# Dilated attention in a two-block kernel: score tiles by residue modulo 4, two slots in one unit of work

## What is computed

```python
for g, (window, dilation) in enumerate(DIL_GROUPS):        # (128, 1), (512, 4), (2048, 16)
    hs = slice(g * HEADS_PER_GROUP, (g + 1) * HEADS_PER_GROUP)
    o, lse = dilated_window_attention(q_d[:, hs], k_d[:, hs], v_d[:, hs], window, dilation)
    outs.append(o)
    lses.append(lse)
w_grp = jax.nn.softmax(jnp.stack(lses, axis=0), axis=0)
o_dil = jnp.sum(w_grp[..., None] * jnp.stack(outs, axis=0), axis=0).astype(h.dtype)
...
o_sb = stick_breaking_attention(qkv_s[0], qkv_s[1], qkv_s[2])
y = gate_dil * (o_dil @ w_proj_dil) + gate_sb * (o_sb @ w_proj_sb)
return y @ w_out
```

## Time and profile before

| | us |
|---|---|
| median of 3 runs | 2889.4 (2888.75 to 2892.43) |
| profiled execution | 2897.6 |
| its span, first to last instruction | 2895.8 |
| PE busy | 2758.5 (95%) |
| DVE busy | 1407.1 (49%) |
| ACT busy | 990.7 (34%) |
| POOL busy | 195.5 (7%) |
| TensorE clock granted, mean of the span | 0.976 |

### The profile page before, as it was taken

The page is one execution under the profiler, slowest core; times in us unless marked ns, Lnnn a source line. Parts: engine busy times, 40 slices in busy tenths (PEclk is TensorE's granted clock), DMA queues, the critical chain, the costliest instruction groups (busy, mean ns, idle before and its releaser), DMA issues.

```text
span 2895.8 us, 30679 instructions
## 1 busy us (share of the span) xinstructions
PE 2758.5 (95%) x12252; PEld 2158.3 (75%) x12252; DVE 1407.1 (49%) x1944; ACT 990.7 (34%) x1367; POOL 195.5 (7%) x149
## 2 busy tenths in 40 slices
PE   7997986999999999989999999999999998999998
PEld 6876764888877766668888888888776666788886
DVE  5455985434454344274443554434544434543434
ACT  5444864222231222453222332223312235422222
POOL 0000115000005000010000000000230001000000
PEclk9997997999999999899999999999999999999999
DMA  4128962222232111032222232222321100322222
GB/s 140 54 71 291 419 265 94 95 95 95 91 105 81 66 50 32 8 100 95 95 95 95 86 104 95 95 95 82 108 81 58 44 19 26 116 95 95 95 95 73
DMA packets 86399, 289.03 MB, mean 100 GB/s; under 512 B 10014, under 2 KB 15070, under 8 KB 86254
## 3 DMA queue, kind: packets, MB, share of 16 engines
q1 hardware_dynamic: 79406, 262.81, 26.6%
q0 software_dynamic: 6272, 22.12, 2.0%
q10 hardware_dynamic: 576, 2.10, 0.2%
HBM read 274.40 MB, written 12.58 MB: 99 GB/s over the span
## 4 chain that ended last, share of the span: by engine, by line
PE 90%; DVE 4%; ACT 3%; issue 2%; DMA 1%; POOL 0%; SPq 0%; DVEq 0%; ACTq 0%; POOLq 0%
PE bank_l L442 73%; PE bank_s L1744 2%; PE bank_o L1761 2%; PE bank_l L1185 2%; PE bank_s L1185 1%; DVE w_lo L416 1%; PE bank_t L1772 1%; PE bank_t L442 1%; PE bank_s L1797 1%; PE bank_s L1742 1%; ACT w_hi L411 1%; PE bank_t L1710 1%; PE bank_s L1811 1%; PE bank_o L1826 1%; PE bank_s L1815 1%
## 5 line engine op out<-in xcount | busy, mean ns | idle before, releaser
L442 PE MATMUL bank_l<-xg_hi,w_hi 128*128 128x512 f32 (+1 forms) x2192 | 879.6, 401 | 18.5 <-DVE w_lo L416 14.4
L442 PE MATMUL bank_l<-xg_lo,w_hi 128*128 128x512 f32 (+1 forms) x2192 | 863.9, 394 | 0.0
L442 PE MATMUL bank_l<-xg_hi,w_lo 128*128 128x512 f32 (+1 forms) x2192 | 858.5, 392 | 0.0
L416 DVE TENSOR_TENSOR w_lo<-w_raw,w_hi 128x1024 fp32r<-128x1024 f32 (+2 forms) x441 | 532.0, 1207 | 227.0 <-ACT w_hi L411 224.9
L411 ACT ACTIVATE w_hi<-w_raw 128x1024 fp32r<-128x1024 f32 (+2 forms) x441 | 435.6, 988 | 434.0 <-PE bank_l L442 418.7
L442 PEld LDWEIGHTS bank_l<-xg_hi,w_hi 128*128 128x128 f32 x2192 | 417.0, 190 | 136.8 <-issue 26.0
L442 PEld LDWEIGHTS bank_l<-xg_lo,w_hi 128*128 128x128 f32 x2192 | 416.1, 190 | 98.2 <-issue 8.4
L442 PEld LDWEIGHTS bank_l<-xg_hi,w_lo 128*128 128x128 f32 x2192 | 417.0, 190 | 90.7
L442 PE MATMUL bank_l<-hid_lo_ff,w_hi 128*128 128x512 f32 x704 | 278.5, 396 | 0.0
L442 PE MATMUL bank_l<-hid_hi_ff,w_lo 128*128 128x512 f32 x704 | 278.5, 396 | 0.0
L442 PE MATMUL bank_l<-hid_hi_ff,w_hi 128*128 128x512 f32 x704 | 278.5, 396 | 0.0
(11 more groups left out here) (331 smaller groups left out, 2821.4 us busy)
## 6 DMA issues: line engine op xcount, KB each, us to landing
w_raw<-in_ff_gate SPq DMA_DIRECT2D x88, 512.0 KB, 3.2
w_raw<-in_ff_up SPq DMA_DIRECT2D x88, 512.0 KB, 3.2
expert_raw<-in_experts SPq DMA_DIRECT2D x81, 512.0 KB, 6.6
w_raw<-in_in SPq DMA_DIRECT2D x80, 512.0 KB, 3.2
w_raw<-in_ff_down SPq DMA_DIRECT2D x64, 512.0 KB, 3.2
w_raw<-in_out SPq DMA_DIRECT2D x24, 512.0 KB, 3.3
w_raw<-in_ff_down SPq DMA_DIRECT2D x32, 384.0 KB, 3.0
y_rows<-y_slot_tile POOLq DMA_DIRECT2D x16, 512.0 KB, 6.6
```

What stands on the lines that cost most here:

```text
L416: dve.tensor_tensor(w_lo[:, i % SPLIT, 0:kc * cols], panel_memory(i), w_hi[:, i % SPLIT, 0:kc * cols].bitcast(F32), ALU.subtract).then_inc ...
L442: done = pe.matmul(dst, w[:, i % SPLIT, c * cols:(c + 1) * cols], moving, start=c == 0 and n == 0, stop=c == kc - 1 and n == 2)
```

## The change

A unit is now a **pair** of slots and a block of queries: eight units for each layer instead of sixteen, with two fillers in each. Within a block of 128 queries the tokens of the second and third group are ordered by their residue modulo 4 (four classes of 32), and the keys and values of these groups by residue over the whole sequence (four classes of 128). A query reads only keys of its own class, so its scores in such a group are one tile of 128, whatever the block. The scores of a slot now fill one bank of 512: 256 keys of the first group, 128 each of the second and third.

- PE: no mask matmuls. For the first group one matmul of 256 columns for each slot of the pair (z = 0, 1), for the others 16 matmuls with 64 rows, 32 columns of weights and 128 columns moving, alternating between the two slots, each to its own 32 partitions of the bank.
- DVE adds a mask in fp32 (`far_masks`, 1 MB, loaded by POOL's queue at the start of each mixer) and takes the maximum in one `tensor_tensor_reduce` for each slot, from PSUM to `prob`. It is built as two instructions. The weights are no longer scaled: the heads are (`take_heads`).
- ACT takes one exponential of 512 for each slot, from SBUF, and copies the weights of z = 0 out of PSUM; DVE copies those of z = 1.
- PE transposes eight blocks (six in the first block) in a row. Its value matmuls have the weights stationary and 64 columns of values moving, so the heads come out token by token: for each slot two of 128 weight columns and eight of 32 weight columns, each with its own 32 partitions. The values of unit u-2 stand behind the transposes of unit u-1. Odd and even units have PSUM banks of their own.
- The heads go to `o_tok` (memory of `squares`). After the last unit the first stick-breaking head waits for it, and PE turns them back with eight transposes (`turn_heads`) behind that head's filler. ACT and DVE split them there (`round_heads`, `rest_of_heads`). The stick-breaking heads are split straight from `bank_o` one by one. `o_f` is gone.
- POOL writes the product with `cos` to a buffer of its own (`turning`), and adds ten of the twelve chunks in the order of the classes: it reads contiguously and writes 32 or 128 elements apart. DVE takes four of the value panels in that order too.
- The bf16 masks of the program's start shrink from 11 tiles to one, and a matmul of one column (L1817) is gone.

```diff
...
-        o += [(f"in_{l}", i) for i in (*range(18), 22, 23, *range(18, 22), *range(24, 40))]
+        o += [(f"in_{l}", i) for i in (*range(18), 22, 23, 18, 24, 19, 25, 20, 26, 21, *range(27, 40))]
...
-            o_f = sb(phase, "o_f", [P, 4, T])
...
+                far_masks = sb(att, "far_masks", [P, TB, T])
...
+                    turning = sb(rope, "turning", [P, 2, T])
...
+                        prob = sb(dilated, "prob", [P, 4, T])
+                        prob_t = sb(dilated, "prob_t", [P, 4, T])
+                    spent = sb(work, "spent", [P, 2, 1280])
...
+            o_tok = squares[:, :, :].rearrange("p a (b d) -> p (a b) d", d=2 * P)
...
-        units = [(s, blk) for blk in range(TB) for s in range(SLOTS)]
+        units = [(pair, blk) for blk in range(TB) for pair in range(SLOTS // 2)]
...
+        def near_keys(blk):
+            return max(blk - 1, 0) * P
...
-                for g in range(3):
-                    pe.matmul(bank_s[:, g, 0:w], ident_bf[:, :], masks_f[:, MASK_END[g] - w:MASK_END[g]],
-                              start=True, stop=False)
-                    m = pe.matmul(bank_s[:, g, 0:w], qk[po:po + 64, ch, blk * P:(blk + 1) * P],
-                                  qk[po:po + 64, 6 + ch, k0 * P:(blk + 1) * P], start=False, stop=True)
...
+                    pe.wait_ge(*routed.upto(("peak", l, u - 1, 1)))
+                for z in range(2):
+                    rows = slice(64 * z, 64 * z + 64)
+                    pe.matmul(bank_s[:, z, 0:2 * P], qk[rows, pair, blk * P:(blk + 1) * P],
+                              qk[rows, 6 + pair, near_keys(blk):near_keys(blk) + 2 * P], start=True, stop=True)
+                for g in (1, 2):
+                    for c in range(4):
+                        for z in range(2):
+                            rows, at = slice(64 * z, 64 * z + 64), blk * P + 32 * c
+                            m = pe.matmul(bank_s[32 * c:32 * c + 32, z, (g + 1) * P:(g + 2) * P],
+                                          qk[rows, 2 * g + pair, at:at + 32],
+                                          qk[rows, 6 + 2 * g + pair, c * P:(c + 1) * P], start=True, stop=True)
...
-                for j in range(nb):
-                    m = pe.matmul(bank_o[po:po + 64, 0:P], v2_tok[:, k0 + j, head:head + HEAD],
-                                  prob_t[:, y, j * P:(j + 1) * P], start=g == 1 and j == 0, stop=g == 0 and j == nb - 1)
...
+            def turn_weights(u):
+                pair, blk = units[u]
+                for z in range(2):
+                    pe.wait_ge(*func.upto(("exp", l, u, z)))
+                    t = claim(pe, t_banks, ("pt", l, u, z), turned_out_v if z else turned_out, ("pt", l, u, z))
+                    for j in range(4):
+                        if blk or j != 1:
+                            m = pe.transpose(t[:, j * P:(j + 1) * P], prob[:, 2 * (u % 2) + z, j * P:(j + 1) * P],
+                                             ident[:, :])
+                    m.then_inc(*turned.done(("pt", l, u, z)))
...
+                    dst, weights = out_bank(u)[:, 64 * z:64 * z + 64], prob_t[:, 2 * (u % 2) + z, :]
+                    head = (2 * pair + z) * HEAD
+                    pe.wait_ge(*(turned_out_v if z else turned_out).upto(("pt", l, u, z)))
+                    for j in range(min(blk, 1) + 1):
+                        pe.matmul(dst, weights[:, j * P:(j + 1) * P],
+                                  v2_tok[:, near_keys(blk) // P + j, head:head + HEAD],
+                                  start=j == 0, stop=False, skip_group_check=True)
+                    for g in (1, 2):
+                        for c in range(4):
+                            at = (g + 1) * P + 32 * c
+                            m = pe.matmul(dst[32 * c:32 * c + 32, :], weights[:, at:at + 32],
+                                          v2_tok[:, c, 256 * g + head:256 * g + head + HEAD],
+                                          start=False, stop=g == 2, skip_group_check=True)
...
+            for u in range(n_units):
+                dilated_scores(u)
+                for n in (2 * u, 2 * u + 1):
+                    x_product(pe, filler(l, n), taken, filler(l, n))
                 if u:
-                    dilated_values(u - 1)
-            weigh_values(*owed.pop())
+                    turn_weights(u - 1)
+                if u >= 2:
+                    weigh_values(u - 2)
+            turn_weights(n_units - 1)
...
+            def turn_heads(pair):
+                t = claim(pe, t_banks, ("heads", l, pair), split_lo, ("o", l, pair))
+                pe.wait_ge(*taken.upto(("o", l, n_units - 1)))
+                for blk in range(TB):
+                    m = pe.transpose(t[:, blk * P:(blk + 1) * P], o_tok[:, blk, pair * P:(pair + 1) * P], ident[:, :])
+                m.then_inc(*turned.done(("heads", l, pair)))
...
-                pe.matmul(bank_s[:, 2, 0:1], ident_bf[:, :], masks_f[:, 0:1], start=False, stop=True,
-                          skip_group_check=True).then_inc(*mixed.done(("weights", l, h)))
...
+            def exp_scores(u):
+                for z in range(2):
+                    act.wait_ge(*routed.upto(("peak", l, u, z)))
+                    st, p = stat[:, u % 2, :], prob[:, 2 * (u % 2) + z, :]
+                    act.activation(p, p, ACT.Exp, scale=-1.0, bias=st[:, z:z + 1],
+                                   accum_out=st[:, 2 + z:3 + z]).then_inc(*func.done(("exp", l, u, z)))
...
+            def round_heads():
+                for pair in range(2):
+                    act.wait_ge(*turned.upto(("heads", l, pair)))
+                    act.activation(by_class(o_hi2[:, pair, :], TB)[0], by_class(
+                        t_banks.of(("heads", l, pair))[:, :], TB)[1], ACT.Copy).then_inc(*split_hi.done(("o", l, pair)))
...
+            def round_stick(h):
+                act.wait_ge(*mixed.upto(("o_stick", l, h)))
+                rows = slice(64 * (h % 2), 64 * (h % 2) + 64)
+                round_value(act, ("o_stick", l, h), o_hi2[rows, 2 + h // 2, :], bank_o[rows, :])
...
-            act.wait_ge(*taken.upto(("o_stick", l, 3)))
-            for c in range(4):
-                round_value(act, ("o", l, c), o_hi2[:, c, :], o_f[:, c, :])
+            round_stick(3)
...
+                        order_of = by_class(v2_f[:, n % 2, :], 1)[1] if 14 <= n < 18 else None
+                        take_panel(key, v2_f[:, n % 2, :], order_of)
...
-                dve.tensor_reduce(st[:, 0:1], bank_s[:, 0, 0:w0], AX, ALU.max).then_inc(*routed.done(("near", l, u)))
-                dve.tensor_reduce(st[:, 1:3], bank_s[:, 1:3, 0:w1], AX, ALU.max).then_inc(*routed.done(("far", l, u)))
-                dve.wait_ge(*routed.upto(("far", l, u)))
-                dve.tensor_reduce(st[:, 3:4], st[:, 0:3], AX, ALU.max).then_inc(*routed.done(("both", l, u)))
-                dve.wait_ge(*routed.upto(("both", l, u)))
-                dve.tensor_scalar(st[:, 4:5], st[:, 3:4], -1.0, None, ALU.mult).then_inc(*routed.done(("peak", l, u)))
-                dve.wait_ge(*func.upto(("far", l, u)))
-                dve.tensor_tensor(st[:, 7:8], st[:, 5:6], st[:, 6:7], ALU.add).then_inc(*routed.done(("sum", l, u)))
-                dve.wait_ge(*routed.upto(("sum", l, u)))
-                dve.reciprocal(st[:, 7:8], st[:, 7:8]).then_inc(*routed.done(("one_over", l, u)))
+                if u >= 2:
+                    dve.wait_ge(*turned.upto(("pt", l, u - 2, 1)))
+                for z in range(2):
+                    dve.tensor_tensor_reduce(prob[:, 2 * (u % 2) + z, :], bank_s[:, z, :], far_masks[:, blk, :], -1.0,
...
+                    dve.tensor_tensor_reduce(prob[:, 2 * (u % 2) + z, :], bank_s[:, z, :], far_masks[:, blk, :], -1.0,
+                                             3e38, ALU.add, ALU.min, stat[:, u % 2, z:z + 1]).then_inc(
+                        *routed.done(("peak", l, u, z)))
...
+            def take_heads(u):
+                pair, blk = units[u]
+                dve.wait_ge(*mixed.upto(("o", l, u)))
                 dve.wait_ge(*routed.upto(("one_over", l, u)))
-                dve.tensor_scalar(prob[:, z, 0:w0 + 2 * w1], prob[:, z, 0:w0 + 2 * w1], st[:, 7:8], None,
-                                  ALU.mult).then_inc(*shaped.done(("prob", l, u)))
-
...
-            take_stick(3)
-            for c in range(4):
-                rest_of_value(dve, ("o", l, c), o_lo2[:, c, :], o_hi2[:, c, :], o_f[:, c, :])
...
+            load(pool, "far_masks", far_masks[:, :, :], dram["far_masks"])
...
+                pool.tensor_tensor(turning[:, i % 2, :], qk[:, i, :], cos[:, :], ALU.mult).then_inc(
...
+                dst, a, b = qk[:, i, :], turning[:, i % 2, :], rot[:, i % 2, :]
+                if i not in (6, 7):
+                    blocks = TB if i < 6 else 1
+                    dst, a, b = by_class(dst, blocks)[1], by_class(a, blocks)[0], by_class(b, blocks)[0]
+                pool.tensor_tensor(dst, a, b, ALU.add).then_inc(*paired.done(("qk", l, i)))
...
```

269 lines of the change are left out of this document (130 added, 139 removed).

## The result

The changed kernel takes **2762.0 us** (median of four runs, 2758.6 to 2763.1), the kernel before, run beside it, 2890.9. The ratio is 0.9533, with a 95% interval of 0.9513 to 0.9554: 129 us less. The forecast was 2811 in a range of 2778 to 2852.

What follows compares the result with a forecast made beforehand. PE, busy 95% of the span, was taken to bound the kernel. Two layers at 51.9 us gave 103.8 less, minus 25.6 for clock falls: 78.2 off 2889.4, 2811 us, range 2778 to 2852.

Steps and rivals of the forecast that it cites:

- Near scores: PE's score matmuls of the first group, two slots together: 0.65 us, about half of 1.24, since the slots use different rows.
- The wait before the first stick-breaking scores: The first stick-breaking head waits for DVE's scaling of the last unit: about 0.6 us more a layer.
- the 2.27 us of the earlier trace: PE's wait behind the last head for copy, roundings and rests; the forecast took 2.1 us a layer off there.
- the price of a small matmul: In the new units, records alternating between tiles start 0.035 us apart, against 0.11 for one more ordinary record.
- My terms were 1.26 and 0.70: Per unit: 32 score records of the other groups in 1.26 us, sixteen 32-column value records of a slot in 0.70.
- Half the columns save nothing: Records with 64 moving and 128 weight columns take 0.113 us each, about the 0.11 of those with 128 moving columns.
- I expect about one such fall a unit: Small matmuls bring PE's granted clock down for 3.4 us in each of sixteen units, losing 25.6 us in all.
- 103.8 forecast without the clock: Gain over two layers, 51.9 us each: 50.4 from PE's units, less 0.6 at the first head, plus 2.1 behind the last.
- The clock holds: Rival: the granted clock does not fall in the units, so the whole 103.8 us are gained, 2786 us; chance 0.22.
- Overlap in part: Rival: PE gets instructions no faster than say 0.07 us a record, 2826 us, or 2872 at 0.11; chance 0.18.
- a new tile costs a change of kind: Rival: each two-record matmul on a new tile takes 0.36 us, a unit 15.0, the kernel 2936 us; chance 0.05.
- The slower case: The 2936 us outcome of costly tile changes, left out of the range; it decides from 0.27 us a matmul on.

## Why the prediction was right and wrong

**What was right.** PE bounds before and after. The growth with the block and the masks went, and the changes of kind from 26 to 8 for two slots, where I had written half. DVE's and ACT's work stayed hidden (the pass three times over changed nothing). Near scores at 0.65 (0.63), transposes and near values within 0.15 us. The wait before the first stick-breaking scores came, 0.41 us where I had 0.6. `turn_heads`, 1.03 us, lies in PE's idle time: the first weights start 10.51 us after the first scores in both kernels, and the wait left is 1.46 instead of 2.35. Behind the last head the 2.27 us of the earlier trace rows are gone and the first gated product comes 3.4 us after the values end (I had 3.5). At full clock the heads are 2.3 us shorter by it; I had 2.1. POOL's additions kept their length.

**The step that failed first: the price of a small matmul.** "24 records in 1.09 us, less 0.3, so 0.035 each" took an average distance from rows in which two to four records run at a time, and applied it to a burst on eight tiles and on four. The distance is not a property of the record. Per tile, one record of 32 weight columns costs 0.109 us for 128 moving columns, as alone, and 0.056 for 64, and the tiles run beside one another. By that, 32 records on eight tiles are 4 x 0.109 + 0.16 = 0.60, and 16 on four with 64 columns 4 x 0.056 + 0.14 = 0.36, which is what the rows after show, and what the runs with one column of tiles, with four times the scores and in another order confirm. My terms were 1.26 and 0.70. "Half the columns save nothing" is true of the rows it was read from, with 128 weight columns, and was wrong for the new values with 32. With the transposes (0.87 for 1.02, and fewer of them in the first block) a layer has 30.6 us of attention, not 44: 27 us for both. A hint lay in my own numbers: I halved the near scores because the two slots use different rows, and did not ask how many tiles the far ones use.

**The step that failed next: the clock.** "I expect about one such fall a unit", 25.6 us, from a single fall in the earlier trace rows. None came, in 120.5 us a layer, nor in the units of any other run in which PE does not wait there. The price was right, the count wrong: the heads of this code take 69.7 us without a fall, 72.9 with 6.8 us at 0.5, 74.4 with 10.2 and 77.5 with 17, that is 0.47 us for each us at half clock, 1.6 for 3.4. What I had cited was "busy then, 3.07 of 3.10 us", of a window that begins at 2200.00. The timeline of the kernel before shows what stood just ahead of that window:

```profile
2199.37 0.33 PE L1772 MATMUL bank_t<-ident,prob 128*128 128x128 f32 x1
2200.03 0.40 PE L1761 MATMUL bank_o<-prob_t,vt 128*64 128x128 f32 x2 [0.34 <-DVE o_f L1983]
```

PE had waited 0.34 us for DVE's copy of the heads, in a run of small matmuls. That this wait brought the fall is not shown: the units of the kernel before have ten waits of 0.25 to 0.47 us in two layers and one fall, and without the masks the same ten and none. The new units have no such wait, since the values lag by one pair more and two banks take turns. The falls in the heads tell the same: windows of the changed kernel, ahead of a fall and in it.

```profile
1143.70:1147.10 3.40, 1.95 (x11) 1.40 (x10) 0.00 (x0) 1.36 (x3) 0.00 (x0) 1.00 0.00 0
1147.10:1150.50 3.40, 3.40 (x8) 2.02 (x7) 0.00 (x0) 0.24 (x1) 0.00 (x0) 0.50 0.00 0
```

PE was idle for 1.45 us, then the clock fell. So the clock was a matter of waits, and I had put it down to the matmuls. What stays open: sixteen waits of 0.87 us brought no fall inside the units and one right behind them, sixteen of 1.47 brought four and one, one of 0.34 amid small matmuls was followed by one, one of 0.47 in the kernel before with its own block alone by another, and with the waits of 1.45 in place the heads of four layers went without any fall (both of the run with six additions, one of the run with four times the scores, one of that with the own block). In the units and the heads every fall stands behind a wait, and where there was none there was no fall; which wait does it, no run here tells.

**Smaller terms.** Three came on top. The heads ran at half clock for 27.2 us before and for 17.0 after: 0.47 x 10.2 = 4.8 us, partly chance. The fall in the units of before, 1.6 us, had counted in its 186.7. The tail gave 0.2 a layer more. Against it stand 3.6 us in the stretch that nobody touched.

**The sum again, with the measured terms.** 103.8 forecast without the clock; 26.8 more for the matmuls of the units, and 1.2 for the wait of 0.6 that I had added (the measured 30.6 hold it); 4.8 and 1.6 of clock in the kernel before; 0.4 for the tail; less 3.6 and 1.2 in the stretches not touched: 133.8 of 135.5 between the two profiled executions. Fillers that are 0.05 us shorter each (90.8 against 89.9 us a layer) are the rest. They now stand two in a row; the masks are not the reason, since without them the fillers of the kernel before took 91.0. Between the medians it is 129; the profiled execution of before stood some 7 us above the median of the runs beside the changed kernel.

**The rivals.** "The clock holds" had the mechanism right, at 2786, and was still 24 us short because the burst was mis-sized in it too. "Overlap in part" and "a new tile costs a change of kind" are refuted by the far scores alone: 0.019 us a record. The slower case would have needed 0.27 us a matmul; it is 0.04. I bounded the small records by 0.035 from below, the best row I had, so the range could not hold a result that was better than that; a price below the nearest row should have been in it, since the new burst uses more tiles than any row did.

## What to carry to other kernels

Price small matmuls by tile: count the records of the fullest tile, multiply by what one record of that shape (weight columns as well as moving ones) takes alone, add one change of kind, and read from the trace how many tiles are at work before taking an average distance from it. Then count changes of kind and waits rather than matmuls: a mask that took 0.23 us from start to start cost 0.36, and regrouping the same matmuls gave 0.14 for each change saved in the values (in the heads less, 1.0 us for twelve). A short wait of the engine that sets the time can cost more than its length, because the granted clock may fall behind it; handing a buffer over in pieces, bank by bank, removed 11.8 us of waits and gave 20, 8 of them from the clock.

## What the runs showed of the hardware

- Eight tiles of 64 x 32 and four of 128 x 32 run side by side: starts 0.007 us apart across tiles (up to 0.017 in the later rounds of a burst of 128 records, 0.013 in the other order), 0.109 (128 moving columns) or 0.056 (64) within one, over 128 records as over 32. Records in another order lost 0.04 us of 0.60.
- With 128 weight columns, records of 64 moving columns start 0.11 us apart; with 32 weight columns, 0.056.
- A matmul of two records went by in 0.031 us on average over 64 of them.
- POOL's additions of 128 x 512 take 1.29 us by themselves and 2.14 to 2.3 where they run beside DVE's weight pass; a step of four in what they write makes no difference.
- The granted clock fell to 0.5 in the units only in kernels where PE waited there (waits of 0.34, 0.47 and 1.47 us), and a fall cost 0.47 us for each us of it.
